# Norm factors of the delta output spread ahead of the GLA loop, and the conformer's first gate weights loaded during GLA

## The chip, the cores and the metric

One core of one Trainium2 chip runs one program, one launch. The metric is the device time of a run in microseconds (us). A profiled execution gives a trace beside it; its times count from the first instruction.

## The reference, cut to what matters

One layer of a hybrid decoder is computed for a prompt of 1024 tokens and for 8 samples of 4 tokens each, 1056 tokens together. All is float32.

```python
h = rmsnorm(x, norm_mix_w) * (1 + sc1) + sh1
(dn_qkv, dn_z, ..., gq, gk, gv, gr, glr, conf_in, br_g) = split(h @ w_in)
o_a, dn_S = gated_delta_rule(q, k, v, beta, g, dn_S0)
o_a = o_a * rsqrt(mean(o_a * o_a) + EPS) * dn_norm_w * silu(dn_z)
log_a = log_sigmoid(glr @ gla_gate_w + gla_gate_b) / 16
o_b, gla_S = gla_recurrence(gq, gk, gv, log_a, gla_S0)
ca, cg = split(conf_in)
cv, conf = causal_dwconv(ca * sigmoid(cg), conf0, conf_dw_w, conf_dw_b)
o_c = silu(layernorm(cv))
merged = sum over n of sigmoid(br_g[n]) * (branch[n] @ w_branch[n])
x = x + gt1 * (merged @ w_out)
```

The mean in `o_a` is over the 128 channels of each of the 4 heads. A mixture of 64 experts and a final norm follow.

## The kernel before, in words

`step_program` (L2817) runs the stages in order: the projections, the delta rule, the GLA rule, the conformer with the merge of the three branches, the output projection, routing, the experts. Each stage is a block of five programs, one for each engine, written out by hand in the order in which the engine is to issue; they meet only at semaphores. A block ends when all engines have reached its end (the block's barrier). `fresh_semaphores` (L153) adds a barrier, a clearing of all semaphores by GpSimd, and a second barrier; it stands, among other places, between GLA and the conformer (L2824).

`gla_rule` (L1155) works through the prompt in chunks of 128 tokens. Its loop has nine iterations: eight chunks, and one for the samples. In each iteration TensorE computes the score levels of two pairs of heads (L1304, L1306), turns keys and values (L1312, L1314), then the output and the state update (L1324 to L1328). Behind the loop come the samples' outputs (L1338, L1340) and states (L1349, drained by VectorE at L1595), which SP stores (L1252); SP's program ends by waiting for these stores.

Between these small matmuls TensorE is given other work, the *fill*: a list of units (L1197 to L1204), each for a third (352) of the tokens. A unit is a number of steps, one matmul each, which the trace shows as two records; it fills one of two PSUM banks in turn and may start only when the unit two before it has been drained by ScalarE or VectorE. The units are:

- `gates`, `q`: GLA's forget gates (1 step) and squared norms of the delta queries turned (4 steps)
- `z`: the gate projection of the delta output, 4 tiles of 8 steps, drained by ScalarE's Silu (L1376)
- `sum`: the sums of squares of the delta output (4 steps), drained by VectorE into a tile of 8 rows, `fac` (L1487)
- `spread`: the norm factors in `fac` spread over the 128 channels of a head (1 step, L1284); VectorE multiplies the delta output by them (L1490)
- `sig`, `glu`: the two halves of the conformer's input, 4 tiles each of 8 steps; ScalarE takes the sigmoid (L1381), VectorE the product (L1501)

A norm factor is 1 / sqrt(mean + EPS). ScalarE takes the root (L1413), VectorE the reciprocal (L1570), both in the first iteration, and TensorE's spread waits for it.

The units before the mark `first_units` are done ahead of the loop. The other ones are dealt out to places in the iteration by `GLA_FILL` (L1147): before, 12 steps behind the first pair's scores (h0 and h1), 1 behind the first transposes (t0), 12 and 1 for the second pair, 2 at the end of the iteration: 28. The steps left to the loop are 252, which are nine times 28. ScalarE and VectorE drain at the same named places, in program order, between the steps of the rule: VectorE at t0, at h1 and h3 (before the next chunk's keys, L1518 and L1519), at t1 and at the end. Keys wait for ScalarE's exponentials of the decays (L1386, L1388); GpSimd's queries (L1454) wait for the keys, and L1304 for the queries. When the spread is through, VectorE multiplies all four heads of Silu(z) and the delta output (L1495) and clears the head of the conformer's input (L1498).

SP loads the weights of `z`, `sig` and `glu` through a ring of three tiles (L1242), each as soon as the tile three before it is used up.

`conformer_and_merge` (L1604) goes over 24 items, a branch's tile of 128 output channels each: the gate (48 records of L1727), then the value (L1741), with VectorE's convolution of 31 taps beside them. `load_item` (L1659) loads both weights of an item into rings of two; TensorE waits at L1746 for both loads of the item before it starts the gate. Item 0 and the convolution's state and taps are issued by SP at the start of the block.

Of the kernel before, what the change touches and what calls it, by code (L numbers as in the profile page):

```python
# [15 lines left out]
ACT = mybir.ActivationFunctionType  # L16
# [3 lines left out]
P = 128  # L20
D = 1024
KT = D // P
# [1123 lines left out]

GLA_FILL = (6, 6, 1, 6, 6, 1, 2)  # L1147

# [6 lines left out]
def gla_rule(k):  # L1155
# [33 lines left out]
                                   "head_rows_shifted"))  # L1189
    kdv_zeroed = k.sem("gr_kdv_zeroed")  # L1190
    s0_loaded = [k.sem(f"gr_s0_loaded{h}") for h in range(H)]
# [5 lines left out]
    units = [("gates", 0, c) for c in three] + [("q", x, 0) for x in three] + [("z", 0, c) for c in three]  # L1197
    units += [("sum", 0, c) for c in three] + [("gates", 1, c) for c in three] + [("z", 1, c) for c in three]
    first_units = len(units)
    units += [("z", m, c) for m in (2, 3) for c in three]  # L1200
    units += [("spread", h, c) for h in range(H) for c in three]
    for j in range(CFC):
# [34 lines left out]
    with nc.Block() as block:  # L1237
        @block.sync
        def _(sp):
            for f in range(3, len(tiles)):  # L1240
                sp.wait_ge(filled, last_unit[f - 3] + 1)
                sp.dma_start(ring[:, f % 3], win[:, :, tiles[f]:tiles[f] + P]).then_inc(k.fill_loaded[f % 3], 16)  # L1242
            sp.wait_ge(L_filled, 4 * NC)
            for h in range(H):
                sp.dma_start(S0[h], a["state_gla"][0, :, h].rearrange("b d e -> d b e")).then_inc(s0_loaded[h], 16)
            sp.wait_ge(S_drained, NC + 1)
            for h in range(H):
                r = slice(64 * (h % 2), 64 * (h % 2) + 64)
                sp.dma_start(a["prompt_state_gla"][0, 0, h], S[h // 2][r, h % 2, :]).then_inc(stored, 16)
            for h in range(H):  # L1250
                sp.wait_ge(S_drained, NC + 1 + 2 * (h + 1))
                sp.dma_start(a["sample_state_gla"][0, :, h].rearrange("b d e -> d b e"), S0[h]).then_inc(stored, 16)  # L1252
            sp.wait_ge(stored, 16 * 2 * H)

        @block.tensor
# [97 lines left out]
        def _(act):  # L1353
# [37 lines left out]
            for h in range(H):  # L1391
                act.activation(sq[:, h, :], src[:, h, :], ACT.Square).then_inc(squared, 1)
            drain(ends[order["gates", 1, NCH - 1]])
            decays(0, 0)
            drain(first_steps)
            act.sem_inc(O_drained, 1)
            decays(0, 1)
            for i in range(NC + 1):
# [11 lines left out]
                drain(points[i, "t1"])  # L1410
                if i == 0:
                    act.wait_ge(by_dve, drains("sum"))
                    act.activation(fac[0:8, :], fac[0:8, :], ACT.Sqrt).then_inc(rooted, 1)  # L1413
                act.wait_ge(O_filled, i + 1)
# [51 lines left out]
        def _(v):  # L1466
# [3 lines left out]
            def drain(to):  # L1470
                while done[0] < len(units) and ends[done[0]] <= to:
# [17 lines left out]
                    elif kind == "spread":  # L1489
                        v.scalar_tensor_tensor(src[:, y, cs], src[:, y, cs], weight, ps[:, bank, 0:CW], ALU.mult, ALU.mult).then_inc(by_dve, 1)  # L1490
                        if (y, c) == (H - 1, NCH - 1):
                            v.wait_ge(by_dve, nth[u])
                            v.wait_ge(by_act, drains("z", 3))
                            for h in range(H):
                                ins = v.tensor_tensor(z[:, h, :], z[:, h, :], src[:, h, :], ALU.mult)  # L1495
                            ins.then_inc(oa_done, 1)
                            v.wait_ge(oa_done, 1)
                            st(v.memset(glu[:, :, 0:CFK], 0.0))  # L1498
                    else:
                        v.wait_ge(by_act, nth[u - 1])  # L1500
# [49 lines left out]
            v.memset(S[0][:, :, :], 0.0)  # L1550
            v.memset(S[1][:, :, :], 0.0).then_inc(S_drained, 1)
            for p in range(2):
                keys(0, p)
            for i in range(NC + 1):
# [12 lines left out]
                drain(points[i, "t1"])  # L1567
                if i == 0:
                    v.wait_ge(rooted, 1)
                    v.reciprocal(fac[0:8, :], fac[0:8, :]).then_inc(inverted, 1)  # L1570
                v.wait_ge(S_filled, i + 1)
# [30 lines left out]


def conformer_and_merge(k):  # L1604

# [4 lines left out]
    glu = glu_tiles(k)  # L1610
    w = Area(k.work[:, 8 * T + CFC * (CFK + T):])
    ring_g, ring_v = w.take(2, KT, P), w.take(2, 4, P)
    cs, before, taps = w.take(SB, CFK + SL), w.take(CFC, SB * CFK), w.take(CFK + 1, CFC)
# [45 lines left out]
    def load_item(sp, q):  # L1659
        m, n = ITEMS[q]  # L1660
        s = q % 2
        c0 = COL["br"] + n * D + m * P
        sp.dma_start(ring_g[:, s], win[:, :, c0:c0 + P]).then_inc(w_loaded[s], 16)
        sp.dma_start(ring_v[:, s], wb[n][:, :, m * P:(m + 1) * P]).then_inc(w_loaded[s], 16)

    with nc.Block() as block:  # L1666
# [29 lines left out]
        def _(pe):  # L1696
# [48 lines left out]
            for q in range(NI):  # L1745
                pe.wait_ge(w_loaded[q % 2], 32 * (q // 2 + 1))  # L1746
                gate(q)
                if q == 0:
                    pe.wait_ge(st_loaded, 48)
                    for m in range(2):  # L1750
# [1066 lines left out]
def step_program(nc, a):  # L2817
    with ExitStack() as ctx:
# [4 lines left out]
        gla_rule(k)  # L2823
        k.fresh_semaphores()  # L2824
        conformer_and_merge(k)
# [32 lines left out]
```

## Time and profile before

| | before |
|---|---|
| median of 3 runs | 2903.79 us (2902.07 to 2907.25) |
| the profiled execution | 2909.69 us, its span 2907.9 us |
| mean granted TensorE clock over the span | 0.97 of 2.4 GHz |
| VectorE, ScalarE, GpSimd busy | 36%, 20%, 28% |
| GLA block, from the first matmul to VectorE's last update | 657.7 to 969.8 us |
| conformer, first to last matmul | 980.4 to 1530 us |

A busy share is an average over all stages, so a stage is read by the timeline (instructions in order of time, with the idle time before each and what ended it) and by windows (busy time of each engine in a stretch). Times of the timeline are starts and durations; a row of several instructions gives their number behind an x. PE is TensorE, PEld its weight loads, DVE VectorE, ACT ScalarE, POOL GpSimd, and SPq the queue of SyncE, which issues the transfers. The granted clock is 1.00 at 2.4 GHz and 0.50 at 1.2 GHz.

### The profile page before, as it was taken

Reading aid. Unit: us, or ns where it says so; the run is one execution under the profiler, and the core shown is the slowest. Engines: PE = TensorE matmul, PEld = TensorE weight load, DVE = VectorE, ACT = ScalarE, POOL = GpSimd, SP = SyncE. Lnnn points to the kernel's source line nnn. Section 1 sums busy time; section 2 is a strip of 40 time slices with the busy share of each in tenths; the row PEclk is TensorE's granted clock in tenths of the full one; section 3 lists DMA queues with packets and bytes.
Section 4 is the critical chain, followed back from the end, with each engine's and each line's share of the span. In section 5 each row is a group of like instructions: output and inputs, shape, how many; then the busy total and the mean of one; then the engine's idle time right before and its main releaser. Section 6 shows DMA issues by size and latency. Waiting matters only on the chain. (4 is left out here: it accounts for less than half of the span.)

```text
span 2907.9 us, 31449 instructions
## 1 busy us (share of the span) xinstructions
PE 2759.3 (95%) x10382; PEld 1626.1 (56%) x10383; DVE 1053.4 (36%) x1635; ACT 575.6 (20%) x1080; POOL 809.8 (28%) x992
## 2 busy tenths in 40 slices
PE   7997999999899899999999898999999999999996
PEld 4564888865566556666666566444444444444443
DVE  3333233334765478842111264322222212222224
ACT  3213333325343100011000130111111111111112
POOL 1000222102242000000000003555655555555543
PEclk8998999999999899999999999999999999999997
DMA  6520000021011211211301220688877788887874
GB/s 238 222 99 25 15 16 22 15 73 31 11 30 25 61 33 33 62 33 35 103 22 47 104 103 1 232 274 281 255 237 208 253 302 289 285 265 250 292 242 137
DMA packets 162802, 382.19 MB, mean 131 GB/s; under 512 B 24595, under 2 KB 111711, under 8 KB 134793
## 3 DMA queue, kind: packets, MB, share of 16 engines
q1 hardware_dynamic: 130449, 311.52, 30.1%
q0 software_dynamic: 32256, 69.33, 10.4%
q8 instruction: 66, 1.08, 0.1%
q14 instruction: 31, 0.25, 0.0%
HBM read 339.65 MB, written 72.94 MB: 142 GB/s over the span
## 5 line engine op out<-in xcount | busy, mean ns | idle before, releaser
L2538 PE MATMUL ps<-big 128*128 x1536 | 678.7, 595 | 6.2 <-SPq L2465 5.4
L2538 PEld LDWEIGHTS ps<-big 128*128 128x128 f32 x1536 | 285.5, 191 | 330.7 <-issue 330.7
L2490 POOL DMA_INDIRECT big<-u_rows,big x384 | 393.3, 1024 | 170.3 <-issue 89.6
L1727 PE MATMUL ps<-big 128*128 128x352 f32 x1152 | 346.9, 461 | 11.8 <-DMA big<-in_w_branch 11.8
L2548 PE MATMUL ps<-big 128*128 x768 | 345.3, 592 | 0.8 <-ACT big L2602 0.8
L2643 DVE SCALAR_TENSOR_TENSOR big<-big,ps 128x256 f32<-128x256 f32 x96 | 64.0, 667 | 652.5 <-ACT big L2592 611.4
L1727 PEld LDWEIGHTS ps<-big 128*128 128x128 f32 x1152 | 219.8, 191 | 135.6 <-DMA big<-in_w_branch 12.6
L2548 PEld LDWEIGHTS ps<-big 128*128 128x128 f32 x768 | 145.8, 190 | 184.3 <-issue 184.3
L846 PE MATMUL ps<-big 128*128 128x352 f32 x576 | 205.5, 463 | 2.0 <-DMA big<-in_w_in 1.9
L2506 POOL DMA_INDIRECT y_rows<-big x96 | 155.8, 1623 | 136.3 <-issue 80.4
L1286 PE MATMUL ps<-big 128*128 128x352 f32 x576 | 182.2, 466 | 5.4 <-DVE big L1501 2.7
L1741 PE MATMUL ps<-big 128*128 128x352 f32 x576 | 174.4, 459 | 1.6 <-DVE big L1860 1.6
L509 PE MATMUL ps<-big 128*128 128x352 f32 x576 | 173.8, 462 | 0.0
L1961 POOL MEMSET big<- 128x1 f32 x1 | 0.1, 98 | 608.9 <-POOLq L1666 608.9
L1830 DVE SCALAR_TENSOR_TENSOR big<-big 128x1024 f32<-128x1024 f32 x120 | 154.0, 1284 | 4.7
L2592 ACT ACTIVATE big<-ps 128x256 f32<-128x256 f32 x96 | 36.8, 383 | 598.2 <-PE ps L2538 550.7
L509 PEld LDWEIGHTS ps<-big 128*128 128x128 f32 x576 | 108.9, 191 | 66.5 <-issue 8.1
L1072 POOL TENSOR_TENSOR big<-big,pair 128x512 f32<-128x512 f32 (+1 forms) x58 | 71.5, 1239 | 266.7 <-DVE big L1092 179.5
L1741 PEld LDWEIGHTS ps<-big 128*128 128x128 f32 x576 | 109.4, 190 | 62.6 <-DVE big L1860 1.8
L1286 PEld LDWEIGHTS ps<-big 128*128 128x128 f32 x576 | 107.0, 191 | 61.7 <-DVE big L1501 3.3
L2637 DVE STREAM_TRANSPOSE big<-big 128x1024 f32<-128x1024 f32 x96 | 117.5, 1224 | 17.5 <-DMA big<-u_rows,big 17.5
L1973 PE MATMUL ps<-big 128*128 128x352 f32 x384 | 115.5, 464 | 2.9 <-PEq L1666 2.9
(558 smaller groups left out, 3010.9 us busy)
## 6 DMA issues: line engine op xcount, KB each, us to landing
big<-in_exp_w_gate SPq DMA_DIRECT2D x64, 1024.0 KB
big<-in_exp_w_up SPq DMA_DIRECT2D x64, 1024.0 KB
big<-in_exp_w_down SPq DMA_DIRECT2D x64, 1024.0 KB
big<-in_ada_w SPq DMA_DIRECT2D x24, 1024.0 KB, 8.2
big<-in_w_in SPq DMA_DIRECT2D x48, 512.0 KB, 4.2
big<-in_w_in SPq DMA_DIRECT2D x6, 1024.0 KB, 5.3
big<-in_w_branch SPq DMA_DIRECT2D x24, 256.0 KB, 4.6
big<-u_rows,big POOLq DMA_INDIRECT x384
```

The source lines that it names most:

```text
L509: ins = pe.matmul(ps[:, 3 * u + c, 0:CW], ring[:, s, j, u * P:(u + 1) * P], k.hT[:, j, c * CW:(c + 1) * CW], start=(j == 0), stop=(j == KT ...
L846: ins = pe.matmul(ps[:, F0 + u % 2, 0:CW], ring[:, f % 3, j, :], k.hT[:, j, c * CW:(c + 1) * CW], start=(j == 0), stop=(j == KT - 1))
L1286: ins = pe.matmul(ps[:, bank, 0:CW], ring[:, tile_of[kind, y] % 3, x, :], k.hT[:, x, cs], start=(x == 0), stop=(x == KT - 1))
L1727: ins = pe.matmul(ps[:, c, 0:CW], ring_g[:, q % 2, j, :], k.hT[:, j, c * CW:(c + 1) * CW], start=(j == 0), stop=(j == KT - 1))
L1741: ins = pe.matmul(ps[:, 3 + c, 0:CW], ring_v[:, q % 2, j, :], branch[n][:, j, c * CW:(c + 1) * CW], start=(j == 0), stop=(j == 3))
L1830: v.scalar_tensor_tensor(o, x_in, f, o, ALU.mult, ALU.add)
L1973: ins = pe.matmul(ps[:, 3 * u + c, 0:CW], ring[:, b % 2, j, u * P:(u + 1) * P], k.merged[:, j, c * CW:(c + 1) * CW], start=(j == 0), stop= ...
L2490: g.indirect_dma_start(out=x_rows[:, u, x * 256:(x + 1) * 256], out_offset=None, in_=u_quarters, in_offset=bass.IndirectOffsetOnAxis(idx_i ...
L2506: g.indirect_dma_start(out=k.y_rows, out_offset=bass.IndirectOffsetOnAxis(idx_out[:, u:u + 1], 0), in_=y_out[:, u, :], in_offset=None, bou ...
L2538: ins = pe.matmul(ps[:, 2 + u, :].rearrange("p (g f) -> p g f", f=FF), xT[:, u, j, :], gate_up[:, j], start=(j == 0), stop=(j == KT - 1))
L2548: ins = pe.matmul(ps[:, 5 + half, :], hidT[:, u, j, :], k.ring[:, bass.ds(off + (DOWN + j * D + half * 512), 512)], start=(j == 0), stop=( ...
L2637: v.transpose(xT[:, u, :, :].rearrange("p j (x c) -> p x j c", x=4), x_rows[:, x, :].rearrange("p (x j c) -> p x j c", x=4, j=KT)).then_in ...
```

## The change

The twelve `spread` units move ahead of the mark `first_units`. The root goes ahead of ScalarE's first decays, the reciprocal and the spread ahead of VectorE's first keys. The products L1495 and the clearing L1498 now stand ahead of the first `glu` product. The last number of `GLA_FILL` goes from 2 to 1, so an iteration has 27 steps, for 240 left to the loop.

The gate weights of the conformer's item 0 are loaded by SP in the GLA block, behind the last ring tile. In the conformer SP raises the semaphore of that load by hand, and TensorE waits for the gate's weights alone before the first gate and for the value's weights after it. The `fresh_semaphores` between the two stages goes. `merge_rings` is the place of the conformer's rings, now shared by both functions.

```diff
-GLA_FILL = (6, 6, 1, 6, 6, 1, 2)
+GLA_FILL = (6, 6, 1, 6, 6, 1, 1)
...
-    kdv_zeroed = k.sem("gr_kdv_zeroed")
+    kdv_zeroed, gate_ahead = k.sem("gr_kdv_zeroed"), k.sem("gr_gate_loaded_ahead")
...
     units += [("sum", 0, c) for c in three] + [("gates", 1, c) for c in three] + [("z", 1, c) for c in three]
+    units += [("spread", h, c) for h in range(H) for c in three]
     first_units = len(units)
     units += [("z", m, c) for m in (2, 3) for c in three]
-    units += [("spread", h, c) for h in range(H) for c in three]
...
                 sp.dma_start(ring[:, f % 3], win[:, :, tiles[f]:tiles[f] + P]).then_inc(k.fill_loaded[f % 3], 16)
+            sp.wait_ge(filled, order["gates", 1, NCH - 1] + 1)
+            sp.dma_start(merge_rings(k)[0][:, 0], win[:, :, COL["br"]:COL["br"] + P]).then_inc(gate_ahead, 16)
             sp.wait_ge(L_filled, 4 * NC)
...
             sp.wait_ge(stored, 16 * 2 * H)
+            sp.wait_ge(gate_ahead, 16)
...
             drain(ends[order["gates", 1, NCH - 1]])
+            act.wait_ge(by_dve, drains("sum"))
+            act.activation(fac[0:8, :], fac[0:8, :], ACT.Sqrt).then_inc(rooted, 1)
             decays(0, 0)
             drain(first_steps)
...
                 drain(points[i, "t1"])
-                if i == 0:
-                    act.wait_ge(by_dve, drains("sum"))
-                    act.activation(fac[0:8, :], fac[0:8, :], ACT.Sqrt).then_inc(rooted, 1)
                 act.wait_ge(O_filled, i + 1)
...
-                        if (y, c) == (H - 1, NCH - 1):
-                            v.wait_ge(by_dve, nth[u])
+                    else:
+                        if (y, c) == (0, 0):
+                            v.wait_ge(by_dve, drains("spread", H - 1))
                             v.wait_ge(by_act, drains("z", 3))
                             for h in range(H):
                                 ins = v.tensor_tensor(z[:, h, :], z[:, h, :], src[:, h, :], ALU.mult)
                             ins.then_inc(oa_done, 1)
                             v.wait_ge(oa_done, 1)
                             st(v.memset(glu[:, :, 0:CFK], 0.0))
-                    else:
                         v.wait_ge(by_act, nth[u - 1])
...
             v.memset(S[1][:, :, :], 0.0).then_inc(S_drained, 1)
+            v.wait_ge(rooted, 1)
+            v.reciprocal(fac[0:8, :], fac[0:8, :]).then_inc(inverted, 1)
+            drain(first_steps)
             for p in range(2):
                 keys(0, p)
...
                 drain(points[i, "t1"])
-                if i == 0:
-                    v.wait_ge(rooted, 1)
-                    v.reciprocal(fac[0:8, :], fac[0:8, :]).then_inc(inverted, 1)
                 v.wait_ge(S_filled, i + 1)
...
+def merge_rings(k):
+    w = Area(k.work[:, 8 * T + CFC * (CFK + T):])
+    return w.take(2, KT, P), w.take(2, 4, P), w
...
-        sp.dma_start(ring_g[:, s], win[:, :, c0:c0 + P]).then_inc(w_loaded[s], 16)
+        if q:
+            sp.dma_start(ring_g[:, s], win[:, :, c0:c0 + P]).then_inc(w_loaded[s], 16)
+        else:
+            sp.sem_inc(w_loaded[s], 16)
         sp.dma_start(ring_v[:, s], wb[n][:, :, m * P:(m + 1) * P]).then_inc(w_loaded[s], 16)
...
             for q in range(NI):
-                pe.wait_ge(w_loaded[q % 2], 32 * (q // 2 + 1))
+                pe.wait_ge(w_loaded[q % 2], 32 * (q // 2 + 1) if q else 16)
                 gate(q)
                 if q == 0:
+                    pe.wait_ge(w_loaded[0], 32)
                     pe.wait_ge(st_loaded, 48)
...
         gla_rule(k)
-        k.fresh_semaphores()
         conformer_and_merge(k)
```

## Rows read from the trace of the kernel before

**Rows 1.** The page: TensorE's busy time, share of the span and records.
```profile
PE 2759.3 (95%) x10382; PEld 1626.1 (56%) x10383; DVE 1053.4 (36%) x1635; ACT 575.6 (20%) x1080; POOL 809.8 (28%) x992
```

**Rows 2.** Timeline, TensorE: start us, us, engine line op out<-in xcount [idle before <-releaser]
```profile
699.91 5.00 PE L1286 MATMUL ps<-big 128*128 128x352 f32 x16 [1.41 <-ACT big L1376]
...
705.52 1.83 PE L1304 MATMUL ps<-big 64*128 64x128 f32 x28 [0.60 <-POOL big L1454]
...
754.81 3.89 PE L1284 MATMUL ps<-big,pick 128*128 128x352 f32 x6 [4.58 <-DVE big L1490]
...
823.78 1.83 PE L1304 MATMUL ps<-big 64*128 64x128 f32 x28
...
848.28 1.83 PE L1304 MATMUL ps<-big 64*128 64x128 f32 x28
...
860.47 6.78 PE L1286 MATMUL ps<-big 128*128 128x352 f32 x22
...
869.94 0.86 PE L1286 MATMUL ps<-big 128*128 128x352 f32 x2 [2.70 <-DVE big L1501]
...
924.73 0.31 PE L1304 MATMUL ps<-big 64*32 64x32 f32 x8
```

**Rows 3.** Windows: us, busy (x) PE, PEld, DVE, ACT, POOL; granted clock, DMA share, GB/s.
```profile
729.00:763.00 34.00, 27.29 (x148) 18.23 (x146) 25.61 (x22) 14.90 (x17) 10.43 (x20) 0.90 0.06 16
763.00:785.00 22.00, 14.78 (x66) 9.33 (x64) 17.37 (x22) 2.92 (x6) 8.31 (x19) 0.84 0.00 0
```

**Rows 4.** Timeline, all engines, from the end of GLA to the conformer.
```profile
956.33 2.71 PE L1286 MATMUL ps<-big 128*128 128x352 f32 x4
...
958.97 2.66 PE L1349 MATMUL ps<-big 128*64 128x512 f32 x4
...
960.82 8.99 DVE L1595 SCALAR_TENSOR_TENSOR xT<-xT,carry,ps 64x128 f32<-64x128 f32 x32 [1.21 <-PE ps L1349]
...
974.86 0.39 SPq L1663 DMA_DIRECT2D big<-in_w_in  x1
...
980.41 16.41 PE L1727 MATMUL ps<-big 128*128 128x352 f32 x48 [11.76 <-DMA big<-in_w_branch]
...
984.09 12.17 PEld L1727 LDWEIGHTS ps<-big 128*128 128x128 f32 x41 [0.25 <-issue]
```

**Rows 5.** By line, 968 to 976 us: ns min/median/max, starts; then SP's waits.
```profile
L1237 SPq EVENT_SEMAPHORE  x1: 17/17/17, 973.2 to 973.2; - x1
...
L157 SPq EVENT_SEMAPHORE  x1: 17/17/17, 974.8 to 974.8; - x1
...
SPq L1237 <- DMA out_sample_state_gla<-xT: 2.4, 1, 2.4
```

**Rows 6.** Timeline, other engines, before the loop and in iteration 0.
```profile
693.47 1.08 ACT L1374 ACTIVATE big<-big 128x1056 f32<-128x1056 f32 x1
...
699.38 0.27 DVE L1551 MEMSET carry<- 128x256 f32 x1
...
719.52 1.23 DVE L1518 TENSOR_TENSOR big<-xT,big 128x1024 f32<-128x1024 f32 x1 [3.03 <-ACT big L1388]
...
721.15 2.09 POOL L1454 TENSOR_TENSOR big<-xT,big 128x896 f32<-128x896 f32 x1 [2.22 <-DVE big L1519]
```

**Rows 7.** Timeline, ScalarE and VectorE, iterations 0 to 2.
```profile
729.48 1.28 ACT L1413 ACT_TABLE_LOAD   x1
...
730.77 1.08 ACT L1413 ACTIVATE big<-big 8x1056 f32<-8x1056 f32 x1
...
731.89 6.74 DVE L1570 RECIPROCAL big<-big 8x1056 f32<-8x1056 f32 x1 [0.84 <-ACT big L1413]
...
756.39 0.58 DVE L1490 SCALAR_TENSOR_TENSOR big<-big,prm,ps 128x352 f32<-128x352 f32 x1 [1.15 <-PE ps L1284]
...
757.56 0.58 DVE L1490 SCALAR_TENSOR_TENSOR big<-big,prm,ps 128x352 f32<-128x352 f32 x1 [0.59 <-PE ps L1284]
...
779.78 4.76 DVE L1495 TENSOR_TENSOR big<-big 128x1056 f32<-128x1056 f32 x4
```

More of the change, by code:

```diff
@@ L1610, in conformer_and_merge @@
     glu = glu_tiles(k)
-    w = Area(k.work[:, 8 * T + CFC * (CFK + T):])
-    ring_g, ring_v = w.take(2, KT, P), w.take(2, 4, P)
+    ring_g, ring_v, w = merge_rings(k)
     cs, before, taps = w.take(SB, CFK + SL), w.take(CFC, SB * CFK), w.take(CFK + 1, CFC)
```

## The prediction

> **What bounds the kernel now.** The page comes first: TensorE is busy for 95% of the span [rows 1]. So time is saved only where TensorE idles, runs at half clock, or does work that can go. The conformer behind the change is full of matmuls and the experts behind that wait mostly for matmuls; I therefore treat all that follows the conformer's first matmul as moving with it, and the sum is how much earlier that matmul starts.
>
> The timeline of TensorE comes second [rows 2]. The GLA loop starts at 705.52 (first L1304) and its ninth, short iteration at 924.73: eight iterations in 219.2 us. One without a stall takes 848.28 - 823.78 = 24.50 us, for 28 fill steps and the rule's own matmuls. Eight would be 196.0, so 23.2 us are lost. The marks in brackets say where: 4.58 us before L1284 (the spread), waiting for VectorE, one of several such waits, and 2.70 us at 869.94 waiting for L1501. A fill step is two matmul records; 22 records in 6.78 us make 0.6 us a step. After the wait of 4.58 us six records take 3.89 us, twice as long: half clock.
>
> The windows view confirms it: over the two stretches with the spread the granted clock averages 0.90 and 0.84 of 2.4 GHz, so 1.2 GHz for part of each, and TensorE is busy 27 of 34 and 15 of 22 us [rows 3].
>
> The timeline of the boundary comes last [rows 4]. VectorE's last update ends at 960.82 + 8.99 = 969.81; the next gate matmul starts at 980.41, released by a weight transfer issued after 974.86. The synchronising lines split those 10.6 us [rows 5]: the queue waits 2.4 us for the last state store, the GLA block's own barrier ends at 973.2, the clearing of semaphores and its second barrier at 974.8, and the transfers take the rest.
>
> **The change, part by part.**
>
> *Boundary.* The clearing and both its barriers go, and the first gate's weights are there already. The store wait and the block's barrier stay. TensorE then waits only for a semaphore that SP raises as its first act; SP's first DMA now starts at 974.86, 0.1 us behind the end of its barrier [rows 4, 5]. I put the matmul at 973.4: **-7.0 us**. Bounds: -1.6 (only 973.2 to 974.8 goes) to -7.1. After an idle 11.8 us the conformer's first records ran at half clock until 984.09; after about 5 us I expect the same and take 0 (bound: -1.8). The small weights, convolution state and taps are needed only after the first gate, which lasts 16.41 us: hidden. The later clear may cover more semaphores; 0, as 1.6 us is the whole of one clear.
>
> *Gate transfer during GLA.* One more DMA on SP, behind the last ring tile and ahead of the state loads. Queued behind its wait are only those loads, and its wait (second gates unit) is met hundreds of us earlier. The last ring tile is asked for long before the loop ends and L1304 of the ninth iteration at 924.73 is behind it, so the transfer has some 50 us: **0**. Uncovered it would cost the 5.6 us from 974.86 to 980.41.
>
> *The square root before the first decays.* ScalarE ends its logarithm at 693.47 + 1.08 = 694.55 [rows 6]. A table load of 1.28 and the root's 1.08 [rows 7] are put in, so the exponentials and the Silu behind them come 2.36 us later. The third chunk of z1 waits for the first Silu: it starts at 699.91 + 2.36 = 702.27, idle 3.77 instead of 1.41 us, and its 16 records end at about 707.0. The Trainium skill, "ScalarE: Activation LUTs", section "What ACT_TABLE_LOAD costs", has about 2.66 us for a switch, a drain included, which would make the sum 1.4 us smaller; the rows show 1.28, with the activation directly behind its load (729.48 + 1.28 = 730.76, and it starts at 730.77).
>
> *The reciprocal, 6.74 us on VectorE* [rows 7], starts after the second state memset, 699.38 + 0.27 = 699.65 [rows 6], and ends at 706.4, before z1 does: hidden on TensorE's path. In the loop it had delayed VectorE in iteration 1.
>
> *Twelve spreads before the loop.* Two banks alternate. At half clock matmuls starting at 754.81 [rows 2] reach L1490 at 756.39, 1.58 us, and the next L1490 follows 1.17 us later, which is the matmul time of a unit; so 0.4 us is the way to VectorE, and at full clock about half of each: 0.6 + 0.2. A bank's turn is then 0.8, 0.58 for L1490 [rows 7] and an estimated 0.1 back, as SP needed behind its barrier: 1.48 us for two units, 0.74 each. From 707.0: 0.8 to the first update, eleven further, the last update: 707.0 + 0.8 + 8.1 + 0.6 = 716.5. VectorE's first keys are queued behind it, then GpSimd's queries, then L1304. From the start of keys to the end of queries is 719.52 to 723.24, 3.7 us [rows 6], so L1304 starts at about 720.3 instead of 705.52: +14.8. TensorE idles 3.8 us before z1's third chunk and 4.4 before the loop. Half clock was seen after 4.58, hardly anything after 2.70 [rows 2]; both are nearer 4.58. Six records at 754.81 took 3.89 us instead of some 2, so about 1.8 a time: **+18.4**. Bounds: +14.8 at full clock, or, with the spreads themselves at 1.17 us each, some 5.5 more, +23.9.
>
> *The loop.* 27 steps make an iteration of 24.50 - 0.60 = 23.90, eight 191.2. Will gated products still stall? Each is drained by VectorE at set places. One that ends in the middle of the second 12-step block (places 14 to 16 of an iteration) is drained only after the second heads' masks, and the unit two later needs its bank. Before, products end at loop step 76 + 16k; only k = 5 falls on place 16 of 28, and there is the stall at 869.94, 21.66 us into its iteration, the block having begun at 12.19: 3.0 us lost. After, they end at 64 + 16k with 27 to an iteration: k = 2 falls on 15 and k = 7 on 14, one and two steps (0.6 each) worse: 3.55 and 4.15. k = 8 falls on 3, a near miss, priced 1.1 (bounds 0 to 3). That is 8.8; 1.8 more for a clock drop after the longest. The 4.76 us of VectorE products that followed the spreads [rows 7] now precede the first gated product (iteration 2, place 10); behind them come the keys, before which VectorE waits for ScalarE anyhow, 3.03 us at 719.52 [rows 6]: 0, bound 1.8. In sum 191.2 + 8.8 + 1.8 = 201.8 against 219.2: **-17.4**. Bounds: -28 (no stall) to -10 (a fourth stall and another drop).
>
> *The last iteration.* One step fewer before its second transposes: -0.6. Its two last steps, 956.33 to 958.97 at half clock, stood before the sample-state matmuls that VectorE's last updates wait for; none is left there: -2.6. **-3.2**, bounds -1.5 to -3.3.
>
> **Sum:** -7.0 + 0 + 18.4 - 17.4 - 3.2 = **-9.2 us**. So the spread's move by itself gains hardly 2; the boundary gains most. The profiled execution took 2909.69 us and would take 2900.5. It lies 5.9 above the median of the three runs; as the stages touched are not the ones waiting for expert weights, I take the difference over: 2903.79 - 9.2 = 2894.6.
>
> **The rivals.** *Clock held.* If neither idle stretch nor the longest stall drops the clock, 5.4 us fewer: -14.6, 2889.2. For: 2.70 us hardly did. Against: 4.58 did.
>
> *Spreads at half clock.* The idle before z1's third chunk drops the clock and alternating matmuls don't win it back: L1490 is fed every 1.17 us, as from 756.39 on. 5.5 us more: -3.7, 2900.1. For: that row. Against: the spread would keep TensorE 80% busy at full clock.
>
> *The transfer still ends last.* If TensorE at the boundary still waits for something that SP issues there, the change does not do what it says and only 1.6 us go: -3.8, 2900.0. Against: its first wait counts 16 and SP gives that at once.
>
> *Slower: half clock through iteration 0.* The place is 702 to the end of the first iteration. Starting from -3.7, each us at half clock in the loop costs 0.5. The loop would have to run some 19 us further at 1.2 GHz to lose 9.5 and pass +5.8, and a whole half-clock iteration, 47.8 us instead of 23.9, gives about +18: 2922. For: 0.84 over 22 us. Against: that is only a third of those 22 us, broken by two idle stretches, and iteration 0 has none.
>
> **How the numbers follow.** 0.2% is 5.8 us, about what a measurement of this kernel can tell from no change. Chances: forecast 0.50, clock held 0.22, spreads at half clock 0.16, transfer last 0.06, half clock through iteration 0 0.06. The forecast's own bounds (a stall more or less, the near miss) leave some 0.43 of its 0.50 beyond -5.8; with 0.22, and 0.03 of the third, faster is 0.68. Slower is the last rival, 0.06. Same is the rest, 0.26. The range reaches from below the held clock, 2887, to above the two small gains, 2902; it leaves out the slower case and the tails.
>
> **What would show it.** Right: the conformer's first gate about 3.6 us behind VectorE's last state update, without a DMA as releaser; L1304 first at 720 to 724; no L1284 inside the loop; unstalled iterations of 23.9 us; idle before L1286 for L1501 in iterations 3 and 6; nothing between L1340 and L1349. Wrong: a first L1304 after 727, iterations above 24.5 without a bracketed wait, or a conformer that shifts by another amount than the final time does.

## The result, and the profile after

The changed kernel takes 2911.12 us (median of 22 runs, 2905.95 to 2922.28) against 2904.05 (22 runs) before: a ratio of 1.0022, 95% interval 1.0015 to 1.003. That is some 6 us slower, where 9.2 us faster was forecast. Its profiled execution took 2911.96 us, span 2910.2.

TensorE's timeline of the changed kernel, in the GLA block (lines past the edits have moved by 2 to 11: L1284, L1286, L1304, L1501 are now L1287, L1289, L1307, L1503):

```profile
700.60 7.66 PE L1289 MATMUL ps<-big 128*128 128x352 f32 x16 [3.80 <-ACT big L1379]
708.10 9.24 PE L1287 MATMUL ps<-big,pick 128*128 128x352 f32 x24
722.54 3.36 PE L1307 MATMUL ps<-big 64*128 64x128 f32 x28 [5.20 <-POOL big L1456]
...
748.27 1.83 PE L1307 MATMUL ps<-big 64*128 64x128 f32 x28
...
772.18 1.83 PE L1307 MATMUL ps<-big 64*128 64x128 f32 x28
...
818.38 2.49 PE L1289 MATMUL ps<-big 128*128 128x352 f32 x4 [3.27 <-DVE big L1503]
...
895.08 3.89 PE L1289 MATMUL ps<-big 128*128 128x352 f32 x6 [3.85 <-DVE big L1503]
...
928.52 0.32 PE L1307 MATMUL ps<-big 64*32 64x32 f32 x8
```

Against [rows 2], L1289 (7.66 instead of 5.00 us) and the first L1307 (3.36 instead of 1.83) run at half clock behind their idle times. The spreads stand ahead of the loop, an undisturbed iteration takes 23.91 us (748.27 to 772.18), and TensorE waits for gated products in iterations 3 and 6. The boundary, all engines of the changed kernel:

```profile
957.38 3.57 PE L1343 MATMUL ps<-carry,xT 64*128 64x4 f32 x16
960.88 5.95 PE L1352 MATMUL ps<-big 128*64 128x512 f32 x8
...
965.95 6.71 DVE L1597 SCALAR_TENSOR_TENSOR xT<-xT,carry,ps 64x128 f32<-64x128 f32 x24 [0.24 <-PE ps L1352]
...
976.15 15.90 PE L1737 MATMUL ps<-big 128*128 128x352 f32 x48 [4.65 <-SPq L1673]
...
979.16 12.32 PEld L1737 LDWEIGHTS ps<-big 128*128 128x128 f32 x42 [0.17 <-issue]
```

The gate starts 3.49 us behind VectorE's last update (965.95 + 6.71 = 972.66) instead of 10.6, released by SP's own semaphore and no transfer [rows 4]. So far the change does what it should. The loss is further on, in code that was not touched. First the kernel before, then the changed one; TensorE's timeline in the norm behind the output projection and where the routed tokens are placed:

```profile
1651.89 2.04 PE L1979 MATMUL ps<-big,ones 128*128 128x352 f32 x6 [2.99 <-DVE big L2036]
...
1658.41 2.14 PE L1987 MATMUL ps<-ones,big 1*128 1x1 f32 x18 [2.70 <-ACT big L2015]
...
1687.73 0.65 PE L2173 MATMUL ps<-big,ones 1*128 1x64 f32 x2 [2.45 <-PEq L157]
...
1759.62 5.28 PE L2207 MATMUL ps<-big 128*128 128x264 f32 x16 [3.26 <-DVE big L2376]
...
1786.51 5.49 PE L2207 MATMUL ps<-big 128*128 128x264 f32 x16 [5.02 <-DVE big L2376]
...
1795.26 3.80 PE L2207 MATMUL ps<-big 128*128 128x264 f32 x16 [3.26 <-DVE big L2376]
```

```profile
1647.11 2.96 PE L1990 MATMUL ps<-big,ones 128*128 128x352 f32 x6 [3.00 <-DVE big L2047]
...
1655.32 3.76 PE L1998 MATMUL ps<-ones,big 1*128 1x1 f32 x18 [2.70 <-ACT big L2026]
...
1686.63 0.66 PE L2184 MATMUL ps<-big,ones 1*128 1x64 f32 x2 [3.03 <-PEq L157]
...
1758.13 6.76 PE L2218 MATMUL ps<-big 128*128 128x264 f32 x16 [3.26 <-DVE big L2387]
...
1786.51 6.24 PE L2218 MATMUL ps<-big 128*128 128x264 f32 x16 [5.01 <-DVE big L2387]
...
1796.01 6.60 PE L2218 MATMUL ps<-big 128*128 128x264 f32 x16 [3.26 <-DVE big L2387]
```

In the norm and the placing the idle times and what ends them are the same to 0.01 us; the matmuls behind them are slower. (The line between them is the routing's first matmul.) The windows of those two stretches (us, busy of PE, PEld, DVE, ACT, POOL, then the granted clock, DMA share, GB/s), before and after:

```profile
1651.90:1660.90 9.00, 5.97 (x31) 4.25 (x31) 0.23 (x2) 2.56 (x3) 0.00 (x0) 0.96 0.00 0
1752.50:1840.80 88.30, 75.06 (x280) 54.45 (x280) 28.30 (x35) 8.78 (x14) 27.78 (x20) 0.96 0.15 60
```

```profile
1647.10:1659.40 12.30, 9.27 (x30) 6.71 (x30) 0.23 (x2) 2.56 (x3) 0.00 (x0) 0.68 0.00 0
1751.00:1844.70 93.70, 80.09 (x280) 57.85 (x280) 28.29 (x35) 8.78 (x14) 27.75 (x20) 0.89 0.14 57
```

The granted clock falls from 0.96 to 0.68 and 0.89: more of each stretch at 1.2 GHz. What differs just ahead of routing is the clearing of semaphores on GpSimd (line, engine, operation, count, ns); since the one between GLA and the conformer is gone, it covers the delta rule's and GLA's semaphores too, 135 instead of 51, and the idle time ahead of the first routing matmul is 3.03 us instead of 2.45. Before, then after:

```profile
L156 POOLq EVENT_SEMAPHORE_RANGE_CLEAR  x1: 307/307/307, 1687.1 to 1687.1; - x1
```

```profile
L156 POOLq EVENT_SEMAPHORE_RANGE_CLEAR  x1: 762/762/762, 1685.5 to 1685.5; - x1
```

By stage, from a stage's first matmul to the next one's, for the profiled pair and a second profile of each kernel (from the first experiment):

| us | before | again | after | again |
|---|---|---|---|---|
| first GLA matmul to first gate | 322.7 | 322.4 | 320.2 | 317.8 |
| first gate to the norm's sums (L1979) | 671.5 | 671.6 | 670.9 | 671.1 |
| norm: sums to transposes (L1993) | 9.0 | 8.9 | 12.3 | 12.3 |
| transposes to placing (L2207) | 91.6 | 88.4 | 91.7 | 91.7 |
| placing to the first expert matmul (L2538) | 88.3 | 88.3 | 93.7 | 93.7 |
| sum | 1183.1 | 1179.6 | 1188.8 | 1186.6 |

The sums' means differ by +6.3 us, about what the ratio gives (0.0022 x 2904 us): the first row gives 3.6, the second 0.6, the other three take 3.3, 1.7 and 5.4. The row from the transposes to the placing is no firm difference: the kernel of before has 91.6 us there in one profile and 88.4 in the other. What follows is the experts and the end, where the same kernel's own profiles differ by several us.

### The profile page after: what moved, and what is told of

It reads as the page before. It is cut to its first block and busy times, and to the rows that moved or that the text cites. A ratio compares the mean times of both kernels' runs of the same rounds, so it can differ in the third digit from the quotient of the medians.

```text
span 2910.2 us, 31427 instructions
## 1 busy us (share of the span) xinstructions
PE 2767.9 (95%) x10382; PEld 1631.9 (56%) x10383; DVE 1055.9 (36%) x1635; ACT 575.4 (20%) x1080; POOL 812.6 (28%) x992
## 5 line engine op out<-in xcount | busy, mean ns | idle before, releaser
L2501 POOL DMA_INDIRECT big<-u_rows,big x384 | 393.3, 1024 | 170.0 <-issue 85.5
L1289 PE MATMUL ps<-big 128*128 128x352 f32 x576 | 187.8, 476 | 12.6 <-DVE big L1503 7.6
L1289 PEld LDWEIGHTS ps<-big 128*128 128x128 f32 x576 | 109.1, 195 | 71.0 <-DVE big L1503 9.5
```

Of the source, the lines that this page charges most:

```text
L1289: ins = pe.matmul(ps[:, bank, 0:CW], ring[:, tile_of[kind, y] % 3, x, :], k.hT[:, x, cs], start=(x == 0), stop=(x == KT - 1))
L2501: g.indirect_dma_start(out=x_rows[:, u, x * 256:(x + 1) * 256], out_offset=None, in_=u_quarters, in_offset=bass.IndirectOffsetOnAxis(idx_i ...
```

## The experiments

**Both kernels again, and each half of the change alone.** The halves are the changed kernel with the other half undone:

```diff
 boundary_only
-GLA_FILL = (6, 6, 1, 6, 6, 1, 1)
+GLA_FILL = (6, 6, 1, 6, 6, 1, 2)
-    units += [("spread", h, c) for h in range(H) for c in three]
     first_units = len(units)
     units += [("z", m, c) for m in (2, 3) for c in three]
+    units += [("spread", h, c) for h in range(H) for c in three]
...
 spread_only
-            sp.dma_start(merge_rings(k)[0][:, 0], win[:, :, COL["br"]:COL["br"] + P]).then_inc(gate_ahead, 16)
...
         gla_rule(k)
+        k.fresh_semaphores()
         conformer_and_merge(k)
```

> The kernel before, unchanged: a second profile, and the noise of the comparison. Both theories: ratio 1.000. In the profiles of before and of the change, the stretch from the conformer's first matmul on costs 8.7 us less and 6 us more than the stages touched explain: the norm's column sums (L1979) ran at full clock in before and at half clock in the changed kernel behind the same idle 3.0 us, and the routing's L2207 likewise. Theory 'stages': that is chance of one execution, so this profile may show the norm stage at 35.8 us (L1979 to L2173) or at some 39. Theory 'phase': whether the clock falls there is set by when the stage is reached, so this profile repeats 35.8 us within 0.5.

> The changed kernel, unchanged: a second profile. Theory 'phase': the norm stage (L1990 to L2184) repeats 39.5 us within 0.5 and routing (L2184 to the first expert matmul behind the block's barrier) 143.8 us. Theory 'stages': they may come out as in before, 35.8 and 138.8. Both: L1307 first some 66.5 us behind the GLA block's first matmul, the conformer 320 us behind it; ratio 1.002.

> The gate weights fetched during GLA and the clearing of semaphores dropped, the spread where it was. Theory 'stages': the conformer starts 7.1 us earlier than in before, the later clear costs 0.6 us more, ratio 0.9978 (0.997 to 0.9985). Theory 'phase': the later stages give back some 5 to 9 us when they are reached at another time; ratio 0.999 to 1.001.

> The spread ahead of the loop and 27 steps an iteration, the boundary as before. From the changed kernel's trace: loop start 18.7 us later, loop and tail 14.2 us shorter, so the conformer starts 4.5 us later. Theory 'stages': ratio 1.0016 (1.001 to 1.0022). Theory 'phase': anything from 0.999 to 1.0045, as the later stages go.

Ratios to before: again 1.0012 (0.9996 to 1.0027), the change 1.0038 (1.0024 to 1.0053), the boundary alone 0.999 (0.998 to 1.0), the spread alone 1.0032 (1.002 to 1.0044). The spread alone lies above what 'stages' has (1.0016) and the boundary alone is where 'phase' has it, though its interval reaches the other. From the norm's sums to the routing the changed kernel repeated its 39.5 us (39.6), as 'phase' asks; the kernel of before did not, with 33.9 instead of 35.8: a miss of 'phase'. There L2001, behind the transposes, took 15.97 us instead of 17.30, and the first routing matmuls were faster too. So one kernel's own executions can differ by some 3 us in such a stretch, and a single profile is to be read with that in mind.

Each half meets one of the two slow stretches. In the timeline of the boundary alone the norm is as before and the placing slow; with the spread alone the other way round:

```profile
1644.90 2.04 PE L1991 MATMUL ps<-big,ones 128*128 128x352 f32 x6 [2.99 <-DVE big L2048]
...
1749.92 6.72 PE L2219 MATMUL ps<-big 128*128 128x264 f32 x16 [3.26 <-DVE big L2388]
```

```profile
1653.14 2.82 PE L1983 MATMUL ps<-big,ones 128*128 128x352 f32 x6 [3.00 <-DVE big L2040]
...
1763.97 5.24 PE L2211 MATMUL ps<-big 128*128 128x264 f32 x16 [3.26 <-DVE big L2380]
```

All profiles together, in us; "cold" is how long the conformer's first weight loads stayed 0.59 us apart, as at half clock, before they closed up (in the changed kernel 979.16 - 976.15 = 3.01):

| kernel | GLA to gate | cold | norm | transposes to placing | clearing | placing | sum |
|---|---|---|---|---|---|---|---|
| before | 322.7 | 3.68 | 9.0 | 91.6 | 0.31 | 88.3 | 1183.1 |
| again | 322.4 | 4.24 | 8.9 | 88.4 | 0.31 | 88.3 | 1179.6 |
| after | 320.2 | 3.01 | 12.3 | 91.7 | 0.76 | 93.7 | 1188.8 |
| again | 317.8 | 3.10 | 12.3 | 91.7 | 0.76 | 93.7 | 1186.6 |
| boundary_only | 316.0 | 4.27 | 8.9 | 89.0 | 0.76 | 93.3 | 1178.9 |
| spread_only | 324.6 | 3.09 | 12.3 | 91.5 | 0.31 | 88.3 | 1187.8 |
| clear_kept | 319.4 | 4.86 | 8.9 | 88.7 | 0.31 | 88.3 | 1177.4 |
| warm_norm | 317.7 | 3.09 | 9.3 | 88.9 | 0.76 | 88.8 | 1175.8 |
| warm_place | 317.7 | 3.09 | 12.3 | 91.8 | 0.76 | 85.5 | 1178.4 |
| fill28 | 310.8 | 3.09 | 12.3 | 91.8 | 0.76 | 93.7 | 1179.8 |
| late1 | 319.0 | 5.39 | 8.9 | 89.3 | 0.76 | 93.8 | 1183.1 |
| late3 | 321.5 | 3.01 | 12.3 | 91.7 | 0.76 | 93.3 | 1189.7 |
| before_warm | 320.1 | 4.27 | 8.9 | 88.4 | 0.31 | 85.1 | 1174.2 |
| after_warm | 319.5 | 3.38 | 9.0 | 92.0 | 0.76 | 87.1 | 1178.8 |
| fill28_warm | 312.5 | 3.38 | 9.0 | 92.0 | 0.76 | 87.1 | 1171.8 |
| before_late7 | 325.8 | 4.24 | 8.9 | 88.4 | 0.31 | 88.4 | 1183.0 |
| before_late8 | 326.9 | 3.03 | 12.3 | 91.5 | 0.31 | 88.1 | 1189.7 |
| before_late9 | 326.1 | 4.85 | 8.9 | 88.8 | 0.31 | 88.3 | 1184.1 |
| before_sems42 | 323.0 | 4.27 | 9.0 | 88.7 | 0.54 | 88.2 | 1180.6 |
| before_sems84 | 322.8 | 3.63 | 12.3 | 91.9 | 0.76 | 93.5 | 1191.8 |

**Is it the clock, and does the clearing matter?** Three edits of the changed kernel:

```diff
 clear_kept
         gla_rule(k)
+        k.fresh_semaphores()
         conformer_and_merge(k)
 warm_norm (project_out, ahead of L1990)
+            for _ in range(4):
+                pe.matmul(ps[:, 6, 0:CW], k.ones[:, :], k.merged[:, 0, 0:CW], start=True, stop=True)
 warm_place (route, ahead of the tile's L2218)
+                for _ in range({1: 4, 4: 7, 5: 4}.get(t, 0)):
+                    pe.wait_ge(q["sh_drained"], 3)
+                    pe.matmul(ps[:, 0, 0:CW], k.ones[:, :], k.hT[:, 0, 0:CW], start=True, stop=True)
```

> The changed kernel with the clearing of semaphores put back between GLA and the conformer; the first gate's weights are still loaded during GLA. Both theories: about 1.6 us more between VectorE's last state update and the first gate than the changed kernel's 3.5, so about 5.1. Theory A (the placing stage ran at 1.2 GHz because the clearing ahead of routing now covers more semaphores and leaves TensorE idle 0.6 us longer): the clearing ahead of routing is back at 0.31 us, the stretch from the first placing matmul to the first expert matmul is back at 88.3 us instead of 93.7, and the stretch from the norm's sums to its transposes stays at 12.3. Rival B (the clock there depends on when the stage is reached, not on the clearing): the placing stretch stays at 93.7, or the norm's stretch changes as well.

> The changed kernel with four more matmuls, whose result nobody reads, in the idle 3 us ahead of the sums of squares of the norm behind the conformer. Theory (that stretch took 3.3 us longer only because TensorE was at 1.2 GHz behind the idle time): L1990, L1993 and L1998 run at their durations of before (2.0, 1.9, 2.1 us) and the stretch from sums to transposes falls from 12.3 to about 9.0 us. Rival (something in that stage waits longer, whatever the clock): it stays at 12.3, with the same releasers.

> The changed kernel with four, seven and four more matmuls, whose result nobody reads, in the idle time ahead of the second, fifth and sixth tile of the placing stage. Theory (5.4 us went to 1.2 GHz in that stage): its matmuls L2218 run at full clock in all tiles and the stretch from the first placing matmul to the first expert matmul falls from 93.7 to 88.3 us or 1 to 3 us below that, since tiles that ran at half clock before the change are at full clock too. Rival (the stage waits for VectorE or the transfers, and the slow matmuls are hidden): it stays within 1 us of 93.7.

Yes: filling the idle time with matmuls brings each stretch back. The timeline of warm_norm (norm and placing), then of warm_place (placing):

```profile
1646.32 2.04 PE L1992 MATMUL ps<-big,ones 128*128 128x352 f32 x6 [0.62 <-DVE big L2049]
...
1751.53 3.80 PE L2220 MATMUL ps<-big 128*128 128x264 f32 x16 [3.26 <-DVE big L2389]
```

```profile
1757.44 3.80 PE L2218 MATMUL ps<-big 128*128 128x264 f32 x16 [0.89 <-DVE big L2390]
```

With warm_place the placing takes 85.5 us. With warm_norm the norm falls to 9.3 us and, unforeseen, the placing to 88.8 with the long clearing still there. So the long clearing makes that stretch slow, but not by itself at any time. clear_kept brings back both, the placing as A has it, and the norm, which only B allows for. One run of each took 2906.07 (clear_kept), 2902.25 (warm_norm) and 2904.47 us (warm_place), beside 2906.77 before; single runs, too few to rank kernels that scatter by several us.

**The places of the gated products.**

```diff
-GLA_FILL = (6, 6, 1, 6, 6, 1, 1)
+GLA_FILL = (6, 6, 1, 6, 6, 1, 2)
```

> The changed kernel with 28 fill steps an iteration again, so that the 240 steps left take eight iterations of 28 and one of 16. Gated products then end at loop steps 64 + 16 k on a period of 28, and only k = 4 falls on place 16. If the places of the products make the stalls, as the prediction had it: one wait for VectorE's gated product of about 3.0 us instead of two of 3.3 and 3.9, in iteration 4, no half clock behind it or for less long, iterations of 24.5 instead of 23.9, and the ninth iteration some 6 us shorter. Sum from the first scores to the samples' outputs: 8 x 24.5 + 3.0 + about 17.5 = 216.5 us instead of 223.4, so about 7 us off, 2904 for the whole if the later stages stay as they are. Rival (stalls come from how long VectorE takes at those points, whatever the place): two or more stalls stay and the stretch is within 2 us of 223.

216.0 us against 222.9 for the second profile of the changed kernel, and one wait, in iteration 4 (besides 0.68 us in iteration 2). TensorE's timeline of fill28:

```profile
788.02 5.59 PE L1289 MATMUL ps<-big 128*128 128x352 f32 x18 [0.68 <-DVE big L1503]
...
844.71 0.93 PE L1289 MATMUL ps<-big 128*128 128x352 f32 x2 [2.70 <-DVE big L1503]
...
846.07 1.38 PE L1289 MATMUL ps<-big 128*128 128x352 f32 x2
```

The reckoning by places holds. Half clock follows the wait all the same: the next fill step (846.07) took 1.38 us where the kernel of before, behind its own wait of 2.70 us, has 0.76, and the granted clock was 0.60 from 844.7 to 848.0 us against 1.00 there. That iteration lost 4.4 us, 1.7 more than its wait. Timed: 2901.75 us, 0.9982 (0.9971 to 0.9993).

**A mere delay.** In the changed kernel, and then in that of before (seven, eight or nine memsets instead of one; three in late3), the first gate waits for memsets of a tile which VectorE clears there anyway:

```diff
+            pe.wait_ge(late, 1)
             for q in range(NI):
...
             st(v.memset(fac[:, :], 0.0))
+            v.sem_inc(late, 1)
```

> The changed kernel, with the conformer's first gate also waiting for VectorE's clearing memset at the start of that block, which it does not need. The first gate starts some 1.3 us later (the memset of the changed kernel began at 976.38 and took 0.94, the gate at 976.15), nothing else is touched. Theory B (the clock of the later idle stretches depends on when they are reached): the 1.3 us don't simply add up; the stretch from the norm's sums to its transposes or the placing stretch changes by 3 to 5 us, and, as in the profiles so far, the norm's stretch is about 9 us if the conformer's first records are at 1.2 GHz for 3.7 us or longer, and 12.3 if for about 3.1. Rival C (it is the code of the changed kernel that slows those stages): norm 12.3 and placing 93.7 as in the changed kernel, and the whole is 1.3 us longer.

> The kernel of before, none of the change in it, with the conformer's first gate also waiting for seven clearing memsets of VectorE (0.94 us each, the first began at 975.16 there) instead of none: the gate starts at about 982.2, some 1.8 us later than before. Theory B (when the later stages are reached decides their clock): with this or with one of the two longer delays the norm's stretch goes from 9 to 12.3 us or the placing stretch from 88.3 to 93.7, with none of the change there. Rival C (the change's code does it): 9 and 88.3 in all three, and each kernel is longer by its delay.

> As the kernel with seven, with eight memsets: the first gate some 2.8 us later than before. Theory B: one of the three has the norm's stretch at 12.3 or the placing stretch at 93.7; where the conformer's first records stay at 1.2 GHz for about 3.1 us the norm's is 12.3, where for 3.7 or longer it is 9. Rival C: 9 and 88.3.

> As the kernel with seven, with nine memsets: the first gate some 3.8 us later than before. Theory B: one of the three has the norm's stretch at 12.3 or the placing stretch at 93.7, the norm's by the same sign at the conformer's start. Rival C: 9 and 88.3.

> The changed kernel with the first gate waiting for three of those memsets instead of one, some 3.2 us later than in the changed kernel. Theory B: the norm's stretch may be 9 or 12.3 and the placing stretch 88.3 or 93.7; the norm's is 12.3 if the conformer's first records are at 1.2 GHz for about 3.1 us, and 9 if for 3.7 or longer. Rival C: 12.3 and 93.7, and the whole 3.2 us longer than the changed kernel.

late1 starts its gate 1.2 us later and has its norm at 8.9 us: 3.4 us back for 1.2. before_late8 has nothing of the change and its norm is slow, before_late7 and before_late9 not. (The gates do not follow in the order of the memsets: they start 325.8, 326.9 and 326.1 us behind the first GLA matmul with seven, eight and nine, as the GLA block itself was shorter in the last.) The norm rows of late8, then of late9:

```profile
1654.74 2.89 PE L1989 MATMUL ps<-big,ones 128*128 128x352 f32 x6 [2.99 <-DVE big L2046]
```

```profile
1655.79 2.04 PE L1990 MATMUL ps<-big,ones 128*128 128x352 f32 x6 [2.99 <-DVE big L2047]
```

So rival C falls for the norm: it is slow without any of the change's code. That it depends on when it is reached is the reading that fits: the sign by the conformer's first records was named before these five ran, and all five have it (cold of 3.01 and 3.03 with 12.3 us, 4.24 and more with 8.9). Each was profiled once, and what sets the moment was not taken apart. The placing did not follow any delay: 93.3 and 93.8 in the changed kernel, 88.1 to 88.4 in that of before.

**The longer clearing alone**, in the kernel of before, by semaphores that nobody uses:

```diff
         conformer_and_merge(k)
+        spare = [k.sem(f"spare{x}") for x in range(84)]
```

> The kernel of before with 84 semaphores more, which nobody uses, so that the clearing ahead of routing covers 135 instead of 51, as in the changed kernel; between GLA and the conformer nothing is changed. Theory A (the longer clearing ahead of routing moves the placing stage to where TensorE falls to 1.2 GHz): the clearing takes 0.76 us instead of 0.31, the idle time ahead of the first routing matmul 3.03 instead of 2.45, the placing stretch 93.7 instead of 88.3, the norm's stretch stays at 9. Theory B alone (only when the conformer is reached decides): 88.3.

> The same with 42 semaphores more: a clearing of about 0.53 us. Theory A: the placing stretch is at one of the two levels, 88.3 or 93.7, or at 90 to 91 if the loss grows with the length of the clearing. Theory B alone: 88.3.

With 84 more the placing takes 93.5 us, with 42 more 88.2: a step, not in proportion. The timeline of before_sems84; the idle time ahead of the routing (L2173) is the changed kernel's 3.03 us, the other two are those of before:

```profile
1650.51 2.65 PE L1979 MATMUL ps<-big,ones 128*128 128x352 f32 x6 [3.00 <-DVE big L2036]
...
1690.19 0.65 PE L2173 MATMUL ps<-big,ones 1*128 1x64 f32 x2 [3.03 <-PEq L157]
...
1761.76 6.81 PE L2207 MATMUL ps<-big 128*128 128x264 f32 x16 [3.26 <-DVE big L2376]
```

Theory A is shown for the placing, with warm_norm as the one case against it: seven of seven profiles with the clearing of 0.76 us and no extra matmuls have it at 93.3 to 93.8, the eight with a shorter one at 88.1 to 88.4. Its norm, expected at 9, came out at 12.3, with nothing edited ahead of it: the gate waited 12.12 us for its transfer instead of 11.76 and 11.49, and cold was 3.63. So the kernel of before can meet that loss by itself. In the sixteen profiles without extra matmuls ahead of the norm, cold of 3.63 us or less went with 12.3 and of 3.68 or more with 9: all sorted, but with a thin gap.

**What is left with both stretches filled.** The extra matmuls of both warm kernels, in the kernel of before, in the changed one, and in fill28:

> The kernel of before with the extra matmuls of both warm kernels (four ahead of the norm's sums; four, seven and four in the placing stage). They can win only what the kernel of before loses to 1.2 GHz there: nothing in the norm's sums, about 1.5 and 1.7 us in two tiles of the placing stage. Stretch from the first placing matmul to the first expert matmul 85.5 instead of 88.3, the whole about 3 us or 0.1% below before.

> The changed kernel with the same extra matmuls. Norm's stretch about 9.3 instead of 12.3, placing 85.5 instead of 93.7, route 61.8 to 64.5. Sum of the stages from the first GLA matmul to the first expert matmul 1172.5 to 1175.5 against 1186.6 to 1188.8 for the changed kernel: the whole 11 to 14 us below the changed kernel, 6 to 9 us (0.2 to 0.3%) below before, and 3 to 6 us below the kernel of before with the same matmuls. If it is not below that one, the change is worth nothing in its own stages either.

> The changed kernel with 28 fill steps an iteration and the extra matmuls. Both savings add: 216.0 from the first scores to the samples' outputs, norm 9.3, placing 85.5; sum of stages 1166 to 1169, the whole 13 to 16 us (0.45 to 0.55%) below before, some 2890 to 2893. Rival: the saved time is given back at another idle stretch that falls to 1.2 GHz instead, and it is no more than 8 us below before.

Ratios to before: 0.9983 (0.9972 to 0.9994), 0.9985 (0.9973 to 0.9997) and 0.9946 (0.993 to 0.9962). after_warm is not clear of before_warm (medians 2898.88 and 2901.06 us, the ratios alike within their intervals), where 3 to 6 us were expected: a miss. In the profiles it has 0.6 us less up to the gate, but 3.6 more from the transposes to the placing and 2.0 more in it, where the extra matmuls do not reach all idle stretches. fill28_warm, 2890.82 us, beats both kernels, though the placing is less good than expected (87.1 us, not 85.5) and the sum of stages is 1171.8 instead of 1166 to 1169.

## Why the prediction was wrong

Taking the profiled pair, in the order of the prediction's sum:

- **Boundary, -7.0:** right, -7.1.
- **Root, reciprocal and spreads, +18.4:** near: the first scores start 66.55 us behind the first GLA matmul (655.99) instead of 47.83, +18.7; in eight of the eleven profiles with this start 65.0 or 65.1, +17.2. The idle times came near the reckoning (3.80 us for 3.77, so the switch of tables cost its load's 1.28 us and no more; 5.20 for 4.4), both with half clock behind them. That behind the second lies in the loop: counted with both, as the sum did, the term is +20.5. The first cost 2.7 us (7.66 for 5.00) and not 1.8, and some 0.9 more went between the first keys and the first scores, where GpSimd's queries overlap the second keys (last section).
- **Loop, -17.4:** -13.2 (722.54 to 928.52 is 206.0). The stalls stand where reckoned, 3.27, 3.85 and 0.43 us for 3.55, 4.15 and 1.1, with one more of 0.40. But 206.0 - 8 x 23.9 - 7.95 leaves 6.85 us: half clock took 1.8 at the start, which the sum had in the term above, 1.7 behind the first stall and 2.7 behind the second, where one drop of 1.8 was in the sum; most of the other 0.6 lies in the two iterations with the short waits. The rival of the held clock had it the wrong way round.
- **Last iteration, -3.2:** -0.9, the worst of the terms in proportion. Four steps went and not three (24 of 28 are left): the one behind the second transposes too, but its time came back as idle time ahead of the samples' outputs (1.93 us for 1.33). The two fill steps at the end went, but they had stood between the samples' small matmuls and their states. In the changed kernel three groups of L1343 took 3.57 us, as the one at 957.38 above, where before two did, and the first states (L1352) ran at half clock as well: eight records took 5.95 us where four later ones took 2.10.
- So the conformer starts 2.5 us earlier (-7.1 + 18.7 - 13.2 - 0.9), not 9.2: the same side, mis-sized by the clock. All of it is the boundary: the spread's move, which the sum had gain 2.2 us (18.4 - 17.4 - 3.2), loses 4.6 in this pair, and about 2 in the spread alone (324.6 us up to the gate against 322.7 and 322.4).

**The step that failed** and turned the sign is the one ahead of the sum: "I therefore treat all that follows the conformer's first matmul as moving with it". It did not. The norm gave back 3.3 us and the placing 5.4, at 1.2 GHz; by the stage table's means 5.6 of the 15.5 us between -9.2 and +6.3 lie ahead of the first gate and 9.9 behind it. For the placing the sum had even named the cause: "The later clear may cover more semaphores; 0, as 1.6 us is the whole of one clear". The clearing did grow by 0.46 us and the idle time ahead of L2184 by 0.58, and with them more of three tiles' matmuls ran at half clock, 1.5, 0.8 and 2.8 us by the rows above; clear_kept and before_sems84 show that the clearing does it. A cost of half a microsecond was priced by its own length and not by what the clock makes of the stretches behind it.

The forecast's slower rival, half clock through iteration 0, was not how it became slower: that iteration took 25.73 us (722.54 to 748.27). The last sign named there, a conformer that shifts by another amount than the final time does, is the one that came.

Left open: what about the moment decides the norm's clock, why the placing's clock follows the clearing and not the delays at the conformer, and why warm_norm undid it. The time from norm to placing is common to both, but no run took it apart.

## What to carry to other kernels

Where TensorE idles for about as long as makes its clock fall sometimes (2.7 to 5 us here), a change far ahead can cost or win several us there without touching it: read the granted clock of every such stretch in both profiles before a difference of a few tenths of a per cent is put down to an edit. Put the price of an added wait into the stages behind it, or fill those idle times with spare matmuls, so that a comparison is not decided by them. And reckon by place and period where a queue written out by hand will stall: the waits' own lengths were forecast to 1 us, and choosing the period by their places (28 instead of 27) was worth 7 us in that stage.

## What the runs showed of the hardware

- The same idle time of 3.0 us ahead of the norm's sums left TensorE at 2.4 GHz or at 1.2 with the same code in that stage: 8.9 to 9.0 or 12.3 us, nothing between in sixteen profiles. The Trainium skill, "TensorE: Matmul & The Clock Gate", Part 1, says that the activity window behind the gate runs freely and is not reset by the kernel; the delays fit that, as eight memsets gave 12.3 and seven and nine 8.9. It also puts the ramp at under 1% of a typical span: the 8.7 us here are 0.3%, and more than the 6 us between the two kernels.
- A wait of 2.70 us in the GLA loop left the granted clock at 1.00 in the kernel before and at 0.60 in fill28, so one case of an idle time that did no harm is no rule.
- The clock also fell while TensorE did not idle: in the kernel before, the samples' groups of 16 records of 4 columns (L1340) took 1.95, 2.58, 3.57 and 3.57 us one behind the other, with a granted clock of 1.00 in the first, 0.73 in the second and 0.50 in the other two, and TensorE busy throughout; 1.33 us of idle time stood ahead of the first.
- Clearing semaphores takes time by their number: 51 in 0.307 us, 93 in 0.542, 135 in 0.762, some 5.4 ns each.
- The norm factors' move lets GpSimd's queries overlap VectorE's second keys: L1456 took 2.99 us instead of 2.08, and L1521, 128 elements, 2.04 instead of 0.29, in the changed kernel's timeline:

```profile
719.50 2.99 POOL L1456 TENSOR_TENSOR big<-xT,big 128x896 f32<-128x896 f32 x1 [19.00 <-DVE big L1521]
720.59 2.04 DVE L1521 TENSOR_TENSOR big<-xT,big 128x128 f32<-128x128 f32 x1
```
